# A two-block hybrid model on one core: a pointwise projection by split weights, row sums finished on TensorE, and outputs evacuated singly

## Time and profile before

| | us |
|---|---|
| median of 3 runs (961.08 to 961.28) | 961.26 |
| the profiled execution's own time | 963.63 |
| its span, first to last instruction | 961.8 |
| TensorE busy in the span | 941.1 (98%), 7136 matmul records |
| VectorE busy | 712.3 (74%) |
| ScalarE busy | 518.9 (54%) |
| GpSimd busy | 15.0 (2%) |
| mean granted TensorE clock | 0.996 |

### The profile page before, as it was taken

One profiled execution on the slowest core, in us unless ns is written; L12 is line 12 of the kernel. 1 busy time (PEld: TensorE's weight loads), 2 busy tenths in 40 slices (PEclk: granted clock), 3 DMA queues, 4 the chain that ended last, 5 costly groups with the idle time before them and its releaser, 6 DMA issues.

```text
span 961.8 us, 19148 instructions
## 1 busy us (share of the span) xinstructions
PE 941.1 (98%) x7136; PEld 906.3 (94%) x7136; DVE 712.3 (74%) x1292; ACT 518.9 (54%) x857; POOL 15.0 (2%) x24
## 2 busy tenths in 40 slices
PE   8999999999999999999999999999999999999997
PEld 6999999999999988899999998999887999999996
DVE  5999999999999647678767445897615888888433
ACT  5547666678665354557554434577213665666320
POOL 0000000000000000000000000000000000000000
PEclk9999999999999999999999999999999999999999
DMA  7576344554554437357555555355046555555501
GB/s 298 178 248 205 117 129 157 196 172 148 182 170 145 168 132 259 136 168 241 181 184 188 176 175 175 117 188 178 2 153 206 187 177 186 184 182 185 201 0 44
DMA packets 45322, 161.50 MB, mean 168 GB/s; under 512 B 5172, under 2 KB 6360, under 8 KB 45144
## 3 DMA queue, kind: packets, MB, share of 16 engines
q1 hardware_dynamic: 43632, 155.01, 47.8%
...
HBM read 159.72 MB, written 1.09 MB: 167 GB/s over the span
## 4 chain that ended last, share of the span: by engine, by line
PE 60%; issue 24%; DVE 10%; ACT 3%; DMA 1%; POOL 0%; DVEq 0%; ACTq 0%; SPq 0%; POOLq 0%
PE A L374 9%; PE A L376 9%; PE A L375 9%; PE B L558 5%; PE B L376 5%; PE B L374 5%; PE B L375 5%; PE A L387 3%; PE B L717 3%; DVE w_lo L1132 2%; DVE part L1168 1%; PE B L707 1%; DVE acc L1371 1%; ACT w_hi L753 1%; DMA raw<-in_weights_dram 1%
## 5 line engine op out<-in xcount | busy, mean ns | idle before, releaser
L374 PE MATMUL A<-h_lo,w_hi 128*128 128x256 f32 x1368 | 393.6, 288 | 6.3 <-DVE sc L1676 1.8
L376 PE MATMUL A<-h_hi,w_lo 128*128 128x256 f32 x1368 | 387.8, 283 | 0.0
L375 PE MATMUL A<-h_hi,w_hi 128*128 128x256 f32 x1368 | 387.7, 283 | 0.0
L1132 DVE TENSOR_TENSOR w_lo<-raw,w_hi 128x1024 fp32r<-128x1024 f32 x249 | 302.8, 1221 | 114.3 <-ACT w_hi L753 112.2
L753 ACT ACTIVATE w_hi<-raw 128x1024 fp32r<-128x1024 f32 x249 | 260.6, 1054 | 162.2 <-PE B L376 75.9
L374 PEld LDWEIGHTS A<-h_lo,w_hi 128*128 128x128 f32 x1368 | 262.8, 192 | 10.3 <-issue 4.6
L375 PEld LDWEIGHTS A<-h_hi,w_hi 128*128 128x128 f32 x1368 | 262.9, 192 | 0.3
L376 PEld LDWEIGHTS A<-h_hi,w_lo 128*128 128x128 f32 x1368 | 262.7, 192 | 0.0
L376 PE MATMUL B<-hid_hi,w_lo 128*128 (+1 forms) x368 | 104.2, 283 | 0.0
L374 PE MATMUL B<-hid_lo,w_hi 128*128 (+1 forms) x368 | 104.0, 283 | 0.0
L375 PE MATMUL B<-hid_hi,w_hi 128*128 (+1 forms) x368 | 103.2, 280 | 0.0
...
## 6 DMA issues: line engine op xcount, KB each, us to landing
...
```

The costliest lines, as they stand in the source:

```text
L374: mm(dst, wh, lo, start=first, stop=False, skip_group_check=free)
L375: mm(dst, wh, hi, start=False, stop=False, skip_group_check=free)
L376: return mm(dst, wl, hi, start=False, stop=last, skip_group_check=free)
L1132: V.tensor_tensor(w_lo[:, s, :], raw[:, s, :], w_hi[:, s, :].bitcast(F32), ALU.subtract).then_inc(lo_ready, 1)
```

## The change

1. The 8 pointwise pieces become split pieces. ScalarE writes the high part of the operand (`conv_hi`), VectorE the low part (`conv_lo`), and VectorE splits weights PW0 to PW0+5 between the steps of the layer norm. The first two pieces run together, chunk by chunk (`two_pieces`); so do the first two mix pieces.
2. The gates' sigmoid is taken as the last gate pieces are drained, and for the first eight once they are all there.
3. At the four residual seams VectorE adds six squares only; TensorE adds the last two itself, into an accumulator that a matmul of zeros has cleared. The zero matmuls ahead go from 8 to 2 or 4, those behind the sums from 3 to 4.
4. `acc_out(m)` and `acc_out(m+4)` share a bank, and each chunk is drained by itself, with waits of TensorE for the drain of chunk m-4.
5. At the seam before the second up projection the two weight splits move away from between the mean and the norm.
6. In the SC stage the VectorE weight splits come two pieces later.
7. The second up projection uses eight banks; its clearing of the accumulators waits for a drained pair, and the last eight down pieces are written out.
8. The final norm is shared: VectorE makes 5 chunks, ScalarE and GpSimd 3 (ScalarE weighs them and copies the norm out of PSUM, GpSimd multiplies, ScalarE stores).

The diff without its unchanged lines, without the new semaphores:

```diff
@@ -76,7 +76,7 @@
-NATIVE = frozenset(GLU_NATIVE) | frozenset([LOOP0 + 8 * i + n for i in range(GROUPS - 1) for n in OUT_AT]) | frozenset(range(TAIL0, MIX0)) | frozenset(range(OUT2, UP2))
+NATIVE = frozenset(GLU_NATIVE) | frozenset([LOOP0 + 8 * i + n for i in range(GROUPS - 1) for n in OUT_AT]) | frozenset(range(TAIL0, PW0)) | frozenset(range(OUT2, UP2))
@@ -194,6 +194,9 @@
+        conv_hi = sb("conv_hi", [P, KD, T], F32R, s2)
+        sb("conv_gap", [P, KD, PAD], scope=s2)
+        conv_lo = sb("conv_lo", [P, KD, T], F32R, s2)
@@ -251,15 +254,19 @@
-            return B[:, m // 2, (m % 2) * T:(m % 2 + 1) * T]
+            return B[:, m % 4, (m // 4) * T:(m // 4 + 1) * T]
-            return DOWN1 + 2 * KD + (DOWN1_REST * (m | 1) + DOWN1_REST - 1) // 8 + 1
+            return DOWN1 + 2 * KD + (DOWN1_REST * m + DOWN1_REST - 1) // 8 + 1
-            return OUT2 + KSC + (m | 1) + 1
+            return OUT2 + KSC + m + 1
+        def down2_done(m):
+            return DOWN2 + 2 * KD + m + 1
@@ -267,7 +274,12 @@
+        UP2_BANKS = UP1_BANKS[4:] + UP1_BANKS[:4]
+        DVE_OUT = 5
+        out_weighted = stage[:, 0, :], stage[:, 1, :], stage2[:, 0, :]
+        pool_rstd = A[2][:, T:2 * T]
@@ -342,7 +357,7 @@
-            for c in range(KD):
+            for c in range(DVE_OUT):
@@ -362,6 +377,10 @@
+            pool.wait_ge(last_scale, 1)
+            for c in range(DVE_OUT, KD):
+                pool.wait_ge(weighted, c - DVE_OUT + 1)
+                nc.gpsimd.tensor_tensor(m_wide[:, c, :], out_weighted[c - DVE_OUT], rs, ALU.mult).then_inc(pool_out, 1)
@@ -402,21 +421,32 @@
-            def first_two(p, operand):
+            def two_pieces(p, bank0, bank1, hi, lo, ready, n):
-                    pe.wait_ge(operand_ready, operand + k + 1)
-                    for j in range(2):
-                        ins = tile((p + j) % RING, k, h_hi[:, k, :], h_lo[:, k, :], A[j][:, 0:T], k == 0, k == KD - 1)
+                    pe.wait_ge(ready, n + k + 1)
+                    for j, bank in enumerate((bank0, bank1)):
+                        ins = tile((p + j) % RING, k, hi[:, k, :], lo[:, k, :], bank, k == 0, k == KD - 1)
-            def spread_residual(summed_n, norm_n, bank, after=8, norm_bank=A[3]):
-                stay_clocked(bank, 8)
-                summed_squares(summed_n, norm_bank)
-                stay_clocked(bank, 3)
+            def spread_residual(summed_n, norm_n, squares_n, bank, ahead, after=8, norm_bank=A[3]):
+                pe.wait_ge(squares_summed, summed_n)
+                mm(norm_bank[:, 0:TT], zero[:, :].bitcast(F32), zero[:, 0:TT].bitcast(F32), start=True, stop=False,
+                   skip_group_check=True)
+                for t in range(TT):
+                    mm(norm_bank[:, t:t + 1], sq_sum[:, 0, t * P:(t + 1) * P], ones[:, 0:1], start=False, stop=False,
+                       skip_group_check=True)
+                stay_clocked(bank, ahead)
+                for c in (KD - 2, KD - 1):
+                    pe.wait_ge(squares_ready, squares_n + c + 1)
+                    for t in range(TT):
+                        ins = mm(norm_bank[:, t:t + 1], sq_wide[:, c, t * P:(t + 1) * P], ones[:, 0:1], start=False,
+                                 stop=c == KD - 1, skip_group_check=True)
+                ins.then_inc(sums_ready, 1)
+                stay_clocked(bank, 4)
@@ -596,19 +626,23 @@
-            for m in range(KD):
+            pe.wait_ge(drained, 6 * GROUPS + 2 * KD - 1)
+            two_pieces(PW0, ring_bank(64), ring_bank(65), conv_hi, conv_lo, conv_low, 0)
+            for m in range(2, KD):
-                native_piece(PW0 + m, ring_bank(64 + m), acc, conv_operand_ready if m == 0 else None)
-            for m in range(KD):
+                chunk_piece(PW0 + m, 0, ring_bank(64 + m), conv_hi, conv_lo)
+            pe.wait_ge(mix_drained, KD - 1)
+            two_pieces(MIX0, ring_bank(72), ring_bank(73), h_hi, h_lo, operand_ready, KD)
+            for m in range(2, KD):
-                chunk_piece(MIX0 + m, 0, ring_bank(72 + m), h_hi, h_lo, KD if m == 0 else None)
-            spread_residual(3, 11, B[:, 0, :], norm_bank=B[:, 3, :])
+                chunk_piece(MIX0 + m, 0, ring_bank(72 + m), h_hi, h_lo)
+            spread_residual(3, 11, 2 * KD, B[:, 0, :], 2, norm_bank=B[:, 3, :])
@@ -651,11 +685,13 @@
+                if m >= 4 and k == 0:
+                    pe.wait_ge(m_copied, KD + m - 3)
-            spread_residual(5, 13, A[2][:, :])
+            spread_residual(5, 13, 4 * KD, A[2][:, :], 2)
@@ -711,30 +747,45 @@
+                if m >= 4:
+                    pe.wait_ge(x_new, 2 * KD + m - 3)
-            spread_residual(7, 15, A[2][:, :], 5)
-            def up_pair(base, j, turn, read=None, n=None):
+            spread_residual(7, 15, 6 * KD, A[2][:, :], 4, 5)
+            def up2_pair(j, turn):
-                    if n is not None:
-                        pe.wait_ge(read, n)
-                    chunk_piece(base + 2 * j + half_, turn, A[j % 2 * 2 + half_][:, 0:T], h_hi, h_lo)
-            first_two(UP2, ops)
-            up_pair(UP2, 1, 0)
-            for j in range(2, 4):
-                up_pair(UP2, j, 0, pairs_drained, KD + j - 1)
+                    chunk_piece(UP2 + 2 * j + half_, turn, UP2_BANKS[2 * j + half_], h_hi, h_lo)
+            two_pieces(UP2, UP2_BANKS[0], UP2_BANKS[1], h_hi, h_lo, operand_ready, ops)
+            for j in range(1, 4):
+                up2_pair(j, 0)
-                    up_pair(UP2, j, i, pairs_drained, i * 4 + (KD + j - 1))
+                    pe.wait_ge(pairs_drained, i * 4 + (KD + j - 3))
+                    up2_pair(j, i)
+            pe.wait_ge(pairs_drained, KD + KF2 - 2)
-            down_turns(DOWN2, KF2 // 8, ops + KD)
-            spread_residual(8, 16, A[2][:, :], 0)
+            down_turns(DOWN2, 2, ops + KD)
+            for m in range(KD):
+                p = DOWN2 + 2 * KD + m
+                pe.wait_ge(lo_ready, split_order(p))
+                if m == 0:
+                    pe.wait_ge(operand_ready, ops + KD + KF2)
+                if m >= 4:
+                    pe.wait_ge(x_new, 3 * KD + m - 3)
+                for k in range(8):
+                    ins = tile(p % RING, k, hid_hi[:, 2 * KD + k, :], hid_lo[:, 2 * KD + k, :], acc_out(m), False, False,
+                               True)
+                ins.then_inc(pieces_done, 1)
+            spread_residual(8, 16, 7 * KD, A[2][:, :], 4, 0)
+            for t in range(TT):
+                ins = mm(pool_rstd[:, t * P:(t + 1) * P], scale[:, t:t + 1].to_broadcast([P, P]), ident, start=True, stop=True)
+            ins.then_inc(rstd_ready, 1)
@@ -889,10 +940,10 @@
-            def drain_gate(s, n, p):
+            def drain_gate(s, n, p, function=ACT.Identity):
-                F(gates[:, s, :], ring(n), ACT.Identity, bias=col("gate_b", s)).then_inc(drained, 1)
+                F(gates[:, s, :], ring(n), function, bias=col("gate_b", s)).then_inc(drained, 1)
@@ -933,10 +984,12 @@
+                act.wait_ge(conv_operand_ready, c + 1)
+                F(conv_hi[:, c, :], acc[:, c, :], ACT.Copy).then_inc(conv_high, 1)
-                drain_gate(EARLY + n, EARLY + n, p)
+                drain_gate(EARLY + n, EARLY + n, p, ACT.Sigmoid if EARLY + n >= KD else ACT.Identity)
@@ -944,6 +997,8 @@
+                    act.wait_ge(drained, 6 * GROUPS + KD)
+                    F(gates[:, 0:KD, :], gates[:, 0:KD, :], ACT.Sigmoid).then_inc(gates_ready, 1)
@@ -951,9 +1006,6 @@
-            act.wait_ge(drained, 6 * GROUPS + 2 * KD)
-            for h in range(2):
-                F(gates[:, h * KD:(h + 1) * KD, :], gates[:, h * KD:(h + 1) * KD, :], ACT.Sigmoid).then_inc(gates_ready, 1)
@@ -977,11 +1029,11 @@
-                    for p in splits_before(c, out2_done, first, end - 2):
+                    for p in splits_before(c, out2_done, first, end - 1):
-                for p in range(max(end - 2, 0), end):
+                for p in range(max(end - 1, 0), end):
@@ -1094,7 +1146,7 @@
-                    F(tap[half_][:, b, :], A[2 * b + half_][:, 0:T], ACT.Identity, scale=w2).then_inc(tap_ready, 1)
+                    F(tap[half_][:, b, :], UP2_BANKS[2 * j + half_], ACT.Identity, scale=w2).then_inc(tap_ready, 1)
@@ -1113,6 +1165,13 @@
+            for c in range(DVE_OUT, KD):
+                F(out_weighted[c - DVE_OUT], x[:, c, :], ACT.Identity, scale=col("final_g_2", c)).then_inc(weighted, 1)
+            act.wait_ge(rstd_ready, 17)
+            F(rs, pool_rstd, ACT.Copy).then_inc(last_scale, 1)
+            for c in range(DVE_OUT, KD):
+                act.wait_ge(pool_out, c - DVE_OUT + 1)
+                act.dma_start(out[:, c, :], m_wide[:, c, :]).then_inc(stored, 16)
@@ -1464,19 +1523,30 @@
+            for p in range(PW0, PW0 + 3):
+                split_lo(p)
+            split_lo(PW0 + 3)
+            split_lo(PW0 + 4)
-            for c in range(KD):
-                V.scalar_tensor_tensor(acc[:, c, :], acc[:, c, :], col("conv_ln_g", c), rstd, ALU.mult,
```

(52 more changed lines are left out.)

3 lines of the change are left out of this document (added).

## The result

The kernel after takes **949.45 us** (median, 949.38 to 949.50), the kernel before, run beside it, 961.27. The ratio is 0.9876 with a 95% interval of 0.9861 to 0.9890: faster, by 11.8 us. The prediction was 947.0 us in a range of 944.7 to 951.7, with a gain of 14.3 us: the sign is right, the time lies inside the range, and the forecast gain is 2.5 us too large. The time is not in the forecast's own case (945.5 to 948.5).

The account below looks back on a forecast made before the run. TensorE was taken to set the time, other engines mattering only where it waits. Gains 4.6 + 1.7 + 0.5 + 0.9 + 1.6 + 3.5 + 1.5 = 14.3 us, from the median 961.26 to 947.0, range 944.7 to 951.7.

Parts of the forecast that it names:

- the forecast's own case: Whole kernel: all parts come as summed, 947.0 us, spanning 945.5 to 948.5; chance 0.60.
- 1, 2: pointwise, with its entry: Pointwise stage: split matmuls take 23.0 us instead of 27.6, gain 4.6; later mean and low parts at entry cost 0.
- 3: mix entry: First two mix pieces: run together, they ask for the late low parts after these arrive; gain 1.7 us.
- 4, and the sums of 5 and 7: Four residual seams: sums end sooner, 1.86 us behind the last tile at the first two; gains 0.5, 0.9, 0.7, 0.66.
- 5: the moved split: Seam before second up projection: moving weight splits away from GpSimd's power cuts it from 1.60 us; gain 0.9.
- 6: SC and LRU gates: SC stage and LRU gates: later splits bring the last SC result before TensorE asks; wait and clock fall go, 3.5 us.
- 7: eight banks: Second up projection: it has no gap to close, so eight banks gain 0.
- 7: the shared final norm: Final norm: chunks and stores shared among engines; 0.84 us of the 1.5 us gain at the end.
- Part 7, the end: Kernel's end: sums to 953.13, GpSimd products 0.69 us each, last store 957.9, end 960.3; gain 1.5 us.
- The SC result did not stay late: Rival, SC stage: ScalarE's high parts keep the result late, the 3.5 us gain is lost, 950.5 us; chance 0.15.
- The pointwise entry held: Rival, pointwise entry: new ScalarE and VectorE work delays it, costing 1 to 3 us, 949.0 us; chance 0.10.
- The clock did not fall in the new seams: Rival, seams: fewer zero matmuls let the granted clock fall, 967.7 us with 45 us of low clock; chance 0.02.

Follow-up runs that it names:

- b_again: The kernel before, run again without edit: 962.52 us median (961.10 to 962.65), ratio 1.0005.
- b_sc_late: The kernel before with only the SC stage's weight splits two pieces later: 959.08 us, ratio 0.9974.
- a_pw_native: The kernel after with the eight pointwise pieces native again: 954.36 us, ratio 0.9930.
- a_mix_single: The kernel after with the first two mix pieces one after the other, not together: 951.04 us, ratio 0.9887.
- a_pairs_sums_old: The kernel after with output chunks drained in pairs and the old order of the sums at all four seams: 951.16 us, ratio 0.9881.
- a_split_back: The kernel after with one weight split back between mean and norm, seam before the second up projection: 950.20 us, ratio 0.9879.
- a_sc_early: The kernel after with the SC stage's weight splits at their old place: 951.31 us, ratio 0.9892; its profiled execution took 952.81.
- a_up_four: The kernel after with its second up projection on four banks again: 949.37 us, ratio 0.9863.
- a_end_dve8: The kernel after with all eight final norm chunks on VectorE and all stores from SyncE: 949.92 us, ratio 0.9875.
- a_next: The kernel after with fewer zero matmuls ahead of the last squares (0, 0, 1, 1) and six final chunks by VectorE: 947.19 us, ratio 0.9841.

## Why the prediction came out as it did

The ledger, each part by the kernel in which it alone is undone, against 949.45. The first column of measured values compares medians. The second compares the profiled executions, each less the time at which TensorE's first tile starts (8.04 us in the kernel after, 7.71 in b_again and b_sc_late, 7.78 to 8.07 in the variants of the kernel after):

| part of the forecast | forecast | by medians | by profiles | kernel |
|---|---|---|---|---|
| 1, 2: pointwise, with its entry | 4.6 | 4.9 | 4.97 | a_pw_native |
| 3: mix entry | 1.7 | 1.6 | 1.69 | a_mix_single |
| 4, and the sums of 5 and 7 | 2.8 | 1.7 | 1.79 | a_pairs_sums_old |
| 5: the moved split | 0.9 | 0.75 | 0.90 | a_split_back |
| 6: SC and LRU gates | 3.5 | 1.9 | with a fall, 3.53 | a_sc_early |
| 7: eight banks | 0 | 0 | 0.01 | a_up_four |
| 7: the shared final norm | 0.8 | 0.5 | 0.50 | a_end_dve8 |
| sum | 14.3 | 11.3 | 13.39 | |

The profiles close: b_again, which has the fall, is 13.39 us longer than the kernel after in the same measure, and b_sc_late, without wait and fall, 9.89, where the parts without part 6 add up to 9.86. By medians it is 11.65 us from the lower level, 961.1, to 949.45, and 0.35 us are in none of the parts. With the start taken out nothing is missing, so they belong to the start as far as one profile for each kernel can tell: TensorE's first tile comes 0.33 us later in the kernel after than in b_again, and 0.1 to 0.3 us later than in most of its variants, so that the medians show the parts and the whole too small. Why the first weights land later there is open.

- **Part 6 is the step that failed.** Its mechanism held: the order of VectorE's splits was the cause, and every link of its chain came as priced (the forecast had the result at 673.9; moved by the 8.25 us by which the first tile behind the FFN's seam is earlier, that is 665.65, and it came at 665.71). Its size did not, for it added two things of different standing: the wait, 1.9 us on both levels, and the clock fall, 1.6 us in about half of the executions. Subtracting both from a median of executions without the fall counts 1.6 us too much. The text had the warning in hand: the profiled execution stood 2.4 above the median. Of those 2.4 us the fall explains 1.5 (the two levels), and the start, 1.0 us longer than in the other profile of this kernel, accounts for the rest. The prediction treated 963.63 - 14.3 and 961.26 - 14.3 as the same subtraction; they weren't. The first, 949.3, was meant for an execution like the profiled one and came within 0.2 us of the profiled 949.5, but by luck: parts that were 0.9 us too large in sum were nearly made up for by the 0.7 us at the start, which no part held.
- **Parts 4, 5 and 7, the sums.** Forecast 1.86 us behind the last tile, measured 2.09; at the two last seams 2.33 and 2.54. The step "0.09 us a record" came from four sums in a row of an old seam. Here four of them take 0.45 us to the next start, not 0.36, the last eight 0.81, not 0.72, and the two zeros 0.55, not 0.46: each change from one kind of matmul to the next costs about 0.09 that the step left out. The clearing takes 0.14, not 0.18. That is 0.2 us a seam, four times. The rest of the 1.1 us lies at the hand-over to the seams: with the sums and the drains undone, the third seam's zeros start 130.6 us behind the first tile after the FFN's seam (593.49 to 724.10), in the kernel after 130.8 (592.69 to 723.50).
- **Part 1** was 0.3 us too cautious, and not on the native side: 27.6 us, 0.43 a matmul, was right. The split matmuls of this stage follow each other at 0.118 us, not at the 0.120 taken from the up projection, so 192 of them take 22.7 us in place of 23.0. The mix pieces of the same kernel stand at 0.120. Why the pointwise ones are faster is open.
- **Part 7, the end.** GpSimd's products were right (0.70 for 0.69). The last one ends 4.77 us behind the sums, as forecast (4.74). What was too small is the last store. The forecast took 2.4 us from a product to the landing, as SyncE's last store has it in the earlier trace rows from the start of its issue (959.4 to 961.8: issue 0.45, landing 1.95 us behind it). ScalarE's last store takes 2.71 us: its issue ends 0.38 us behind the product (945.37 against 944.99), and the span ends 2.33 us behind that. The three stores of ScalarE's queue land 2.2 to 2.3 us behind their issues, the eight of SyncE's in the kernel before 1.9 to 2.1. The Trainium skill's GPSIMD Engine Reference (section 3.1), scaled by elements, had given an estimate of 0.56 us a product; the trace says 0.70.
- **The rivals.** The SC result did not stay late, and came 1.0 us ahead of the piece that needs it (665.71 against 666.73). The pointwise entry held with 0.3 us to spare. The clock did not fall in the new seams, nor in those of a_next (1.00 in both profiles).

What stays open: that the upper level of the kernel before is the clock fall rests on the profiles of three executions with the fall (two of the kernel before, one of a_sc_early), each on an upper level, and on its absence without the wait; no profile of a lower-level execution with the wait was taken. Nor is it known why one stand of 1.9 us brings the fall and the next does not. Its length alone does not decide: in the profile of the kernel before TensorE stood 2.35 us for its first weights at the start, and the matmuls behind that stand took 0.38 us each, as long as the native ones elsewhere at full clock.

## What to carry to other kernels

Ask of every stall in a profile whether it is in the median as well: compare the profiled execution with the runs, find the difference (here 1.0 us at the start and 1.5 of clock) and leave it out of the sum before subtracting from a median. When parts undone one by one do not add up to the whole, compare their profiles from the first useful instruction on; here the missing 0.35 us lay ahead of it. Two parts of a change that shorten the same chain are not to be added; undo both and each of them. When TensorE turns over zeros to wait for others, take away zeros until it waits: the last square showed the limit in one row.

## What the runs showed of the chip

- A stand of TensorE of 1.9 us in a kernel that was otherwise at full clock goes with two levels of time, 1.5 us apart (961.1 and 962.5, 22 and 25 of 48 executions). In the three profiles of an upper level the granted clock falls behind the stand, 0.3, 1.3 and 1.2 us after TensorE has started again, to the level of 1.2 GHz (0.52 over the 3.3 us of the earlier trace rows); each variant that removes the stand has a single level, but for one execution each of b_sc_late (960.05) and a_pw_native (956.86), which no profile explains.
- A GpSimd instruction of two elements per partition takes 0.69 us beside an idle VectorE. Where a VectorE instruction with two tensors from SBUF began 0.16 us ahead of it, it ended 0.54 to 0.55 us behind that instruction: 0.86 us in all beside one of 0.48, 1.60 beside one of 1.2, and no more when a second one of 1.2 us followed.
- GpSimd multiplies two float32 tiles of 128x256 from SBUF in 0.70 us, one after the other, while VectorE multiplies a tile from SBUF by one from PSUM for most of that time; that product of VectorE's takes 0.41.
- A store of 128 KB landed 1.9 to 2.1 us behind the end of its issue from SyncE's queue in the kernel before, and 2.2 to 2.3 us from ScalarE's queue in the kernel after, where SyncE's five, issued at the same time, took 1.9 to 2.6.
